# Inverse roots of the head norms as exp(-0.5 ln x) on the scalar engine, with the row stores and value-row copies on other engines

## The reference

```python
def rms_norm(x, g):
    xf = x.astype(F32)
    y = xf * lax.rsqrt(jnp.mean(xf * xf, axis=-1, keepdims=True) + EPS)
    return (y * g.astype(F32)).astype(x.dtype)

k, v = jnp.split(h @ w_kv, [N_HEADS * 2 * HEAD_DK], axis=-1)
k = rms_norm(k.reshape(bsz, L, N_HEADS, 2, HEAD_DK), k_norm)     # returned, and used
q = rms_norm((h @ w_q).reshape(bsz, L, N_HEADS, 2, HEAD_DK), q_norm)
...
o = rms_norm(o, subln) * (1.0 - lam_init)                        # o of the attention, per head
return o.reshape(bsz, L, N_HEADS * HEAD_DV) @ w_o
```

## Time and profile before

| what | value |
|---|---|
| median of three runs | 2074.89 us |
| the profiled execution | 2083.15 us, of which its span 2081.3 us |
| PE busy / PEld busy | 1851.6 us (89%) / 1659.0 us (80%) |
| DVE busy | 839.7 us (40%) |
| ACT busy | 734.0 us (35%) |
| POOL busy | 142.5 us (7%) |
| L1761, reciprocals of 128x576 on DVE | 24, 3748 ns each, 90.0 us |
| L1231, square roots of 128x576 on ACT | 24 |
| loads of ACT's function tables, whole program | 26, 1283 ns each |

### The profile page before, as it was taken

How to read it: one execution, slowest core, us unless ns; L and a number is a source line. 1 busy time by engine, 2 the same in 40 slices (tenths; PEclk the granted TensorE clock), 3 DMA queues, 4 the chain that set the end, 5 groups by cost and what they waited for, 6 DMA issues and landing times.

```text
span 2081.3 us, 42740 instructions
## 1 busy us (share of the span) xinstructions
PE 1851.6 (89%) x17223; PEld 1659.0 (80%) x17223; DVE 839.7 (40%) x1423; ACT 734.0 (35%) x1112; POOL 142.5 (7%) x277
## 2 busy tenths in 40 slices
PE   4798889899999999898868888988758799999998
PEld 2473679799999999798856766666438799999997
DVE  6557223433333233315764444444454433333232
ACT  1433333433333222424346444444131333333212
POOL 2010012200000022101010000000013200000000
PEclk9878899899999999899989999999868799999999
DMA  8758642122222223222158888888651122222222
GB/s 241 261 186 285 210 134 81 51 78 84 81 81 76 70 83 96 61 81 61 61 170 278 324 317 310 306 305 303 217 162 51 51 81 81 81 81 70 82 83 73
DMA packets 245005, 301.03 MB, mean 145 GB/s; under 512 B 10188, under 2 KB 195472, under 8 KB 244816
## 3 DMA queue, kind: packets, MB, share of 16 engines
q1 hardware_dynamic: 241752, 290.22, 42.5%
q10 hardware_dynamic: 2432, 8.16, 1.1%
q0 software_dynamic: 704, 0.95, 0.2%
HBM read 291.92 MB, written 7.37 MB: 144 GB/s over the span
## 4 chain that ended last, share of the span: by engine, by line
PE 71%; DVE 10%; DMA 7%; ACT 4%; SPq 4%; issue 3%; POOL 0%; DVEq 0%; ACTq 0%; POOLq 0%
PE ps L576 55%; PE ps L499 5%; DMA kpg<-in_cache_k 3%; DVE t L1761 2%; SPq L449 2%; DMA raw<-in_w_ada_mix 2%; PE ps L526 2%; SPq L456 2%; PE ps L860 2%; PE ps L715 1%; DMA vpg<-in_cache_v 1%; PE ps L931 1%; DMA raw<-in_w_ada_ffn 1%; ACT kTs L1341 1%; DVE wh L1701 1%
## 5 line engine op out<-in xcount | busy, mean ns | idle before, releaser
L576 PE MATMUL ps<-hr,ws 128*128 128x288 f32 x5760 | 787.2, 299 | 34.8 <-DVE hr L1719 16.9
L576 PEld LDWEIGHTS ps<-hr,ws 128*128 128x128 f32 x5760 | 782.6, 192 | 38.7 <-issue 31.4
L1713 DVE TENSOR_TENSOR ws<-raw,ws 128x1024 fp32r<-128x1024 f32 x200 | 234.8, 1176 | 699.9 <-ACT ws L1189 699.9
L1189 ACT ACTIVATE ws<-raw 128x1024 fp32r<-128x1024 f32 x200 | 201.2, 1008 | 656.9 <-PE ps L576 632.0
L576 PE MATMUL ps<-gr,ws 128*128 128x288 f32 x2112 | 279.4, 294 | 0.0
L576 PEld LDWEIGHTS ps<-gr,ws 128*128 128x128 f32 x2112 | 279.1, 188 | 0.0
L1341 ACT ACTIVATE kTs<-ps 128x512 f32<-128x512 f32 x256 | 141.2, 596 | 165.5 <-PE ps L499 165.1
L499 PE MATMUL ps<-ident,kpg 128*128 128x128 f32 x1024 | 152.7, 298 | 15.7 <-DMA kpg<-in_cache_k 10.6
L499 PEld LDWEIGHTS ps<-ident,kpg 128*128 128x128 f32 x1024 | 123.1, 152 | 46.6 <-issue 23.1
L526 PE MATMUL ps<-raw,cond 128*32 128x256 f32 x896 | 83.5, 482 | 44.7 <-DMA raw<-in_w_ada_mix 34.6
L576 PE MATMUL ps<-hg,ws 128*128 128x288 f32 x768 | 106.2, 302 | 8.9 <-DVE ws L1713 8.9
(11 more groups left out here) (312 smaller groups left out, 1595.2 us busy)
## 6 DMA issues: line engine op xcount, KB each, us to landing
kpg<-in_cache_k SPq DMA_DIRECT2D x128, 512.0 KB, 5.7
vpg<-in_cache_v SPq DMA_DIRECT2D x128, 512.0 KB, 5.9
raw<-in_ffn_w SPq DMA_DIRECT2D x88, 512.0 KB, 3.8
raw<-in_w_ada_mix SPq DMA_DIRECT2D x48, 512.0 KB, 5.4
raw<-in_w_ada_ffn SPq DMA_DIRECT2D x48, 512.0 KB, 4.8
raw<-in_ffn_w SPq DMA_DIRECT2D x48, 384.0 KB, 3.5
raw<-in_w_ada_kv SPq DMA_DIRECT2D x16, 512.0 KB, 5.6
raw<-in_ssm_w_glu SPq DMA_DIRECT2D x16, 512.0 KB, 4.3
```

What stands on the lines that cost most here:

```text
L576: return mm(ps[:, 4 * s + 2 * tile + h, 0:HALF], ws[:, (u * S + j) % 2, w, k, :], src[:, k0 + k, v, h * HALF:(h + 1) * HALF], start=(k0 + ...
L1189: A(ws[:, w, 0, 0:nk, :].rearrange("p k n -> p (k n)"), raw[:, slot, 0:nk, :].rearrange("p k n -> p (k n)"), ACT.Copy).then_inc(slab_high, 1)
L1713: TT(f(ws[:, w, 1, 0:nk, :]), f(raw[:, slot, 0:nk, :]), f(ws[:, w, 0, 0:nk, :]).bitcast(F32), ALU.subtract).then_inc(raw_done[slot], 1)
```

## The change

Three edits.

1. `head_root` no longer takes a square root. ACT takes the logarithm of mean plus epsilon, waits for it by a new semaphore `ln_head`, and takes exp(-0.5 ln), in place in `t2[:, s]`. VectorE's `head` loses the reciprocal and its step. It holds for k, q and the attention's output, 24 heads.
2. The ten stores of the token rows are issued by GpSimd, each after `free[s]` of its turn, between its part of the modulation for q and its wait for the last head of q. The stores of y stay with ACT and count on a semaphore of their own, `y_put`.
3. The rows of v (turns 5 to 9) are copied out of PSUM by VectorE, after the head of the same turn. The last of them first waits for five stores out of `tok_put[0]`.

```diff
             def head_root(n, bank, s, width):
                 act.wait_ge(head_ready, n + 1)
-                return A(halves(t2[:, s, :]), ps[:, bank:bank + 2, 0:HALF], ACT.Sqrt, bias=eps[:, 0:1], scale=1.0 / width)
+                A(halves(t2[:, s, :]), ps[:, bank:bank + 2, 0:HALF], ACT.Ln, bias=eps[:, 0:1], scale=1.0 / width).then_inc(ln_head, 1)
+                act.wait_ge(ln_head, n + 1)
+                return A(t2[:, s, :], t2[:, s, :], ACT.Exp, scale=-0.5)
...
-                if v and i < QB:
-                    dst = vtok[:, i].rearrange("p h d -> p (h d)")
-                else:
-                    dst = tok[0:NTOK[i], slot, :]
-                    if v or i >= 2:
-                        act.wait_ge(tok_put[slot], 16 * (3 + 2 if v else i // 2))
-                A(dst, ps[0:NTOK[i], 4 * s + 2:4 * s + 4, :].rearrange("p b c -> p (b c)"), ACT.Copy).then_inc(free[s], 1)
+                if not v:
+                    if i >= 2:
+                        act.wait_ge(tok_put[slot], 16 * (i // 2))
+                    A(tok[0:NTOK[i], slot, :], ps[0:NTOK[i], 4 * s + 2:4 * s + 4, :].rearrange("p b c -> p (b c)"), ACT.Copy
+                      ).then_inc(free[s], 1)
                 if n + 2 < H:
                     square(qT, n + 2, s)
-                act.wait_ge(free[s], uses("qtok", s, n // 2) + 1)
...
-                act.dma_start(rows_.rearrange(form), dst).then_inc(tok_put[slot], 16)
...
@@ gpsimd
             apply("q")
+            for n in range(2 * (QB + 1)):
+                s, v, i = n % 2, n // (QB + 1), n % (QB + 1)
+                pool.wait_ge(free[s], uses("qtok", s, n // 2) + 1)
...
+                dst = vtok[:, i].rearrange("p h d -> p (h d)") if v and i < QB else tok[0:NTOK[i], i % 2, :]
+                pool.dma_start(rows_.rearrange(form), dst).then_inc(tok_put[i % 2], 16)
             pool.wait_ge(head_ready, 2 + 2 * H)
...
@@ vector
             def head(src, h, s, g):
-                step(REC(t2[:, s, :], t2[:, s, :]))
                 t = tile(src, h)
                 STT(t, t, g, t2[:, s, :], ALU.mult, ALU.mult).then_inc(head_ready, 1)
...
-            for n in range(H):
-                dve.wait_ge(root_head, n + 1)
-                head(qT, n, n % 2, vec[:, 121:122])
+            for n in range(2 * (QB + 1)):
+                s, v, i = n % 2, n // (QB + 1), n % (QB + 1)
+                if n < H:
+                    dve.wait_ge(root_head, n + 1)
+                    head(qT, n, s, vec[:, 121:122])
+                if v:
+                    wait_unit(dve, "qtok", s, n // 2)
+                    dst = vtok[:, i].rearrange("p h d -> p (h d)") if i < QB else tok[0:NTOK[i], i % 2, :]
+                    if i == QB:
+                        dve.wait_ge(tok_put[i % 2], 16 * 5)
+                    CP(dst, ps[0:NTOK[i], 4 * s + 2:4 * s + 4, :].rearrange("p b c -> p (b c)")).then_inc(free[s], 1)
...
-            with step.loop(0, H // 2, 2) as i:
+            with dve.Fori(0, H // 2) as i:
```

More of the change, by code:

```diff
@@ L315, in yoco_step @@
         e_ready, g_high, g_ready = sems("e_ready g_high g_ready")
-        sq_head, root_head, head_ready, blocks_ready = sems("sq_head root_head head_ready blocks_ready")
-        tok_put = pair("tok_put")
+        sq_head, ln_head, root_head, head_ready, blocks_ready = sems("sq_head ln_head root_head head_ready blocks_ready")
+        tok_put, y_put = pair("tok_put"), pair("y_put")
         tri_ready, s_full, s_max, e_done, w_done, wp_turned, wp_copied, pv_full, head_out = sems(
@@ L491, in _ @@
             for s in range(2):
-                sp.wait_ge(tok_put[s], 16 * 3 * (3 - s))
+                sp.wait_ge(tok_put[s], 16 * (6, 4)[s])
+                sp.wait_ge(y_put[s], 16 * (3, 2)[s])
         @block.tensor
@@ L1390, in _ @@
                 if i >= 2:
-                    act.wait_ge(tok_put[s], 16 * ((6, 4)[s] + i // 2))
+                    act.wait_ge(y_put[s], 16 * (i // 2))
                 A(tok[0:NTOK[i], s, :], ps[0:NTOK[i], 4 * s:4 * s + 2, :].rearrange("p b c -> p (b c)"), ACT.Copy
@@ L1395, in _ @@
                 act.dma_start(out[0][0, i * P:(i + 1) * P] if i < QB else out[1].rearrange("b t d -> (b t) d"),
-                              tok[0:NTOK[i], s, :]).then_inc(tok_put[s], 16)
+                              tok[0:NTOK[i], s, :]).then_inc(y_put[s], 16)
         @block.gpsimd
@@ L1514, in _ @@
             apply("q")
+            for n in range(2 * (QB + 1)):
+                s, v, i = n % 2, n // (QB + 1), n % (QB + 1)
+                pool.wait_ge(free[s], uses("qtok", s, n // 2) + 1)
+                o_ = out[6 + v] if i < QB else out[8 + v]
+                rows_ = (o_[0, i * P:(i + 1) * P] if i < QB else o_)
+                form = {(0, 0): "t h m d -> t (h m d)", (0, 1): "t h d -> t (h d)", (1, 0): "b t h m d -> (b t) (h m d)",
+                        (1, 1): "b t h d -> (b t) (h d)"}[(int(i == QB), v)]
+                dst = vtok[:, i].rearrange("p h d -> p (h d)") if v and i < QB else tok[0:NTOK[i], i % 2, :]
+                pool.dma_start(rows_.rearrange(form), dst).then_inc(tok_put[i % 2], 16)
             pool.wait_ge(head_ready, 2 + 2 * H)
@@ L1767, in dense @@
                 S, n0 = len(slabs), SLABS[name] - DENSE0
-                steps_ = per * {"glu": 1, "q": 1}.get(name, 0)
+                steps_ = per * {"glu": 1}.get(name, 0)
                 def turn(i, last):
```

4 lines of the change are left out of this document (removed).

## The result

The changed kernel takes **2092.39 us** (median of 4 runs, 2089.26 to 2093.55); the kernel before, run beside it, takes 2074.97 us (4 runs, 2073.44 to 2076.32). The ratio is 1.0082, with a 95% interval from 1.0064 to 1.0099: slower by 17.0 us (13.3 to 20.5). The forecast was 2094.2 us, with a range from 2085 to 2103 and 90 in 100 for slower. The profiled execution took 2093.55 us, its span 2091.7 us.

The account below looks back on a forecast made before the run. VectorE's reciprocals were taken to bound qtok and ohead, with ACT the bound after the change. Terms of 12.9 (q, qtok, tail), -1.3 (attention) and 7.7 (ohead) gave 19.3 us, so 2094.2 us, range 2085 to 2103.

Parts of the forecast that it names:

- The price of a root on ACT: Head norms on ACT: two loads of 1.30 us, logarithm 0.74, exponential 0.69, so 4.03 us from root's end to root's end.
- drain of about 1380 ns: Rival, at 34 loads on the path: 1.38 us more each, 47 us in all, giving 2141 us; 3 in 100.
- q: Stage q: PE stands still 3.2 us longer once at the start; PE's first sum of qtok comes 2.8 us late.
- PE covers the rest: In q after the first gap: a unit takes PE 7.3 us and ACT needs 6.3, so no further loss.
- a dearer tail: Rival: store behind qtok lands after 8.6 us (+4.3), PE's clock falls in q's gap (up to 3): +7.3, 2101.5 us; 12 in 100.
- qtok and the tail: Through qtok to kn: +12.9 us, of which 2.8 from q, about 2 from ACT's period, 8 from behind the last root.
- the two end together: Behind qtok: PE's turns of the first pages, 3.8 us from the last copy, end at the same time as kn comes.
- Attention: Attention: the load before a sequence's first exponential goes, where PE waited 2.1 us for page copies; counted -1.3 us.
- the attention gives the time back: Rival: PE's 10.6 us of page waits in the attention vanish with a later start: 8.7 us, 2083.6; 13 in 100.
- ohead: Stage ohead: ACT becomes the bound at 4.6 to 5.2 us per head, wo starts later: +7.7 us.
- The sum: Whole kernel: 12.9 - 1.3 + 7.7 = 19.3 us slower; applied to the median, 2094.2 us, 0.9% slower.
- The rival without switches: Rival in q, qtok, attention and ohead: both functions share a table, loads go: -21.6 us, 2053.3 us; 7 in 100.

Follow-up runs that it names:

- The load of the active set: Changed kernel with the combined table set loaded by name ahead of each logarithm and each exponential, 48 loads kept: 2094.79 us in one run.
- the own tile: Changed kernel with the last rows of v in their own buffer (no store wait), masks and first kn ahead of GpSimd's last three stores: 2096.65 us.
- roots alone: Kernel before with only the logarithm and exponential replacing root and reciprocal; stores and rows of v stay on ACT: 2096.22 us.
- moves alone: Changed kernel with square root and reciprocal restored; only the stores and the rows of v are moved: 2081.63 us.
- before, exponential's table: Kernel before with one more load, the exponential's table, on ACT behind its last row copy of qtok: 2074.88 us.
- after, one set: Changed kernel with one table set holding both logarithm and exponential loaded by name once, ahead of q's head norms: 2050.92 us.
- after, one set, own tile: Changed kernel with the combined table set loaded once, own buffer for the last rows of v, and masks and first kn ahead of the last stores: 2049.78 us.
- roots alone, one set: Kernel before with logarithm and exponential and their combined table set loaded by name; stores and rows of v stay on ACT: 2046.17 us.
- roots, one set, own tile: Kernel before with logarithm and exponential, their combined set loaded by name, and own buffer for the last rows of v, copied by ACT: 2048.87 us.
- before, late turns: Kernel before with one added wait: PE's turns of the first two half pages begin only when the last head of q is scaled: 2073.96 us.

## Why the prediction was right, step by step

**The price of a root on ACT: right.** Two loads of 1283 ns, an ACTIVATE 0.01 to 0.02 us behind each, logarithm 0.74 and exponential 0.68: 4.03 us from the copy's end to the exponential's end in q, as worked out. ACT's period in qtok was 5.53 (1035.61 to 1041.14, the starts of two loads; 5.5 predicted). The first logarithm of qtok to the last exponential's end took 39.2 us (38.9); the last turn's logarithm waited 0.15 us for PE's rows, where the step had said up to 0.5. The load of the active set shows that nothing is saved by which set it is. The Trainium skill's drain of about 1380 ns beside each load (ScalarE: Activation LUTs, What ACT_TABLE_LOAD costs) would by the estimate in the prediction (34 loads on the path) have added some 47 us to the stages' 20.6, 68 in all; they are 21.7 longer, and no gap stands behind a load. Here the measurement decides against the page.

**q: right in kind, mis-sized.** +4.4 instead of +2.8. The gap of 3.2 us more came (3.97 in all), and the term "PE covers the rest" left out what follows such a gap: 7.76 us for 45 matmuls instead of 6.20, 1.56 us more, with the granted clock at 0.50 for some 3.4 us of them. That was in the rival "a dearer tail", at up to 3 us, and not in the sum.

**qtok and the tail: right.** +9.5, where the forecast had 10.1 (12.9 less the 2.8 of q). From the last exponential's end to the product with kn it was 10.7 us (11.6 predicted). The store landed after 2.9 us, not 4.3; the 0.8 us in that term for its size had no row behind it. Against this gain stand 0.28 us from each copy's end to the issue of its store, twice, which no term had. The turns of the page cost nothing more, since PE waited 0.23 us for kn behind them. The step said that the two end together, which the own tile confirmed: there kn was ready 6 us sooner (47.5 us after qtok's start, not 53.9), and PE began only 1.6 us sooner.

**Attention: right in sign, too small.** I counted -1.3 for the load that goes; the second exponential comes 4.0 us sooner. PE's longest wait for ACT's page copies fell from 2.1 to 0.7 us, as said. But the load's wait had also cost the clock behind it, and it was worth 2.2. And the late kn gave back something that no term had: before, PE had stood still for 3.0 us when kn came, and its clock stayed at 0.50 for 5.5 us more; after, the turns of the page run up to kn and the clock is full 1.5 us behind it. That is worth 2.0 us, and pages took 0.2 of it. In the repeated profile of after, waits for pages left only 1.6 of the 4.0. So the rival "the attention gives the time back" had a part of the truth, by another mechanism than the one it named: the waits for pages in the attention were 10.6 us before and 10.1 after, and 13.1 in the repeated profile. That the attention as a whole was 5.1 us shorter is no evidence for more, since two profiles of before differ by 4.8.

**ohead: right.** +7.8 against +7.7. The last exponential ends at 1575.13 and PE starts wo at 1575.23. (Three times 4.6 and four times 5.2 make 34.6 and not 34.5, which changes nothing.)

**The sum.** The stages and the attention's beginning make 4.4 + 9.5 + 7.8 - 4.0 = 17.7 us; predicted were 19.3, measured by the runs 17.0 (13.3 to 20.5). With the beginning of the repeated profile it would be 20.1. The forecast is better than its terms, and that much is luck: q was 1.6 us too low and the attention 2.7 us too high, which partly cancel. The same count for the other kernels, beside their runs:

```
                              stages  2nd exp    sum    runs
roots alone                    +21.9     -3.4  +18.5    +17.2 (10.6 to 23.7)
moves alone                     +8.8     -2.5   +6.3     +3.5 (-0.4 to 7.5)
after, own tile                +20.1     -4.2  +15.9    +18.5 (12.9 to 24.1)
before, exponential's table      0.0     -2.7   -2.7     -2.1 (-6.2 to 2.1)
after, one set                 -23.7     -3.9  -27.6    -27.4 (-33.0 to -21.8)
after, one set, own tile       -27.2     -4.0  -31.2    -26.1 (-30.7 to -21.8)
roots alone, one set           -26.1     -3.5  -29.6    -31.7 (-36.3 to -27.2)
roots, one set, own tile       -26.9     -4.6  -31.5    -27.6 (-33.0 to -22.2)
before, late turns              +0.6     -1.3   -0.7     -2.1 (-6.0 to 1.7)
```

All but one lie in their interval, and that one is 0.5 us outside.

**The rival without switches** was wrong for this kernel and right about its price: worked out at -21.6 us, found at -27.6 by the stages and -27.4 by the runs once the set was loaded by name. The Trainium skill (ScalarE: Activation LUTs, Table sets: the hidden batching unit) counts one load for a logarithm and an exponential. That is what the chip can do; the built kernel had taken a load for each, and only the set's name in the program made it true.

**Open.** The attention behind its second exponential and the front vary by several us from execution to execution of one kernel; why, and whether the change moves anything there, isn't settled. The table of the beginning was worked out from the traces afterwards, and no run was made to test it; up to 0.5 us between its rows stay unexplained.

## What to carry to other kernels

When a step is rewritten with other functions on ACT, count the table loads between them before anything else: two loads for each root made a bound of an engine with time to spare, and one line that names a set with both functions turned 17 us lost into 27 won. Then look at what stands behind the last turn of a loop: a store that had to land before a buffer was used again held VectorE up for 2.2 us there, and taking the wait away made qtok 1.6 us shorter. And price a gap of the bound engine with what its clock does afterwards, which goes both ways: here a gap of 4 us cost 1.6 more, and with PE at work up to kn, instead of waiting for 3 us, the clock gave back about 2.0.

## What the runs showed of the hardware

- A load of the table set that is already active takes the full 1283 ns, the same as a change of sets (all 48 loads of that run, of which 47 surely follow the same set; total time 2094.79 us).
- The granted TensorE clock fell to 0.50 about 1 us after PE had begun again behind a gap of 3.97 us in q, and stayed there for some 3.4 us. Behind a wait of 2.13 us in the attention it did the same. Behind the wait of 3.02 us for kn, which it had spent at 0.50, it stayed there for 5.5 us more; in the changed kernel, where PE had worked right up to kn, also at 0.50, it was full after 1.5 us.
- A copy of 64x1024 out of PSUM takes VectorE 1.22 us, as long as 128x1024 (1.22 for one, 2.35 for two): here half the partitions save nothing.
- A store of 512 KB issued by GpSimd costs that engine 0.53 us and landed after a median of 2.9 us (2.8 to 4.2), against 2.6 from ACT's queue.
